# Six value products of a head in one run, six transposed-probability buffers, one move of y per head

## What is computed

```
mod = silu(cond) @ w_ada + b_ada                      # six vectors of 1024 per conditioning vector
h = rmsnorm(x, norm1) * (1 + sc1) + sh1
proj = h @ w_in                                       # columns for groups A, B, C, D
y_a = gated width-3 convolution
y_b = softmax attention, 4 latent heads (keys of width 96)
y_c = softmax attention, 4 heads on 2 key heads, with rotary tables
y_d = the same, in a window of 128 tokens, with a sink in the denominator
x = x + g1 * (concat(y_a, y_b, y_c, y_d) @ w_out)
h = rmsnorm(x, norm2) * (1 + sc2) + sh2
x = x + g2 * (gated MLP with a width-3 convolution on h)
```

## Time and profile before

| what | value |
|---|---|
| median of 3 runs | 1806.75 us (1806.15 to 1808.81) |
| the profiled execution: time, span | 1807.65 us, 1805.9 us |
| granted TensorE clock, mean | 0.981 |
| PE busy | 1712.2 us (95%) |
| PEld busy | 1537.8 us (85%) |
| DVE busy | 1114.8 us (62%) |
| ACT busy | 626.3 us (35%) |
| POOL busy | 150.2 us (8%) |
| HBM | 86 GB/s over the span |

### The profile page before, as it was taken

One profiled execution on the slowest core, in us unless ns is written; L12 is line 12 of the kernel. 1 busy time (PEld: TensorE's weight loads), 2 busy tenths in 40 slices (PEclk: granted clock), 3 DMA queues, 4 the chain that ended last, 5 costly groups with the idle time before them and its releaser, 6 DMA issues.

```text
span 1805.9 us, 30070 instructions
## 1 busy us (share of the span) xinstructions
PE 1712.2 (95%) x11625; PEld 1537.8 (85%) x11625; DVE 1114.8 (62%) x2279; ACT 626.3 (35%) x1257; POOL 150.2 (8%) x152
## 2 busy tenths in 40 slices
PE   5899999899999999999989989979999999999997
PEld 3899555469999999999989965545999999999997
DVE  3656666565766566566782856656576565665675
ACT  2421453453432222322242235436243322222223
POOL 0351010120000000000004402011100000000000
PEclk7899999999999999999999999999999999999998
DMA  8331442332222222222312322212223222222211
GB/s 273 110 103 36 143 146 94 117 120 68 71 82 70 80 71 70 81 70 80 89 47 67 95 78 94 94 48 87 89 70 94 71 70 74 77 70 81 70 59 59
DMA packets 188438, 156.53 MB, mean 87 GB/s; under 512 B 7824, under 2 KB 175284, under 8 KB 188340
## 3 DMA queue, kind: packets, MB, share of 16 engines
q1 hardware_dynamic: 188340, 155.19, 28.1%
HBM read 151.86 MB, written 3.31 MB: 86 GB/s over the span
## 4 chain that ended last, share of the span: by engine, by line
PE 85%; DVE 6%; DMA 3%; ACT 3%; issue 2%; POOL 1%; SPq 0%; DVEq 0%; ACTq 0%
PE PS L1106 81%; PE PS L1110 4%; DMA RW<-in_w_ada_dram 2%; DMA RW<-in_w_in_dram 1%; DVE H_lo L1627 1%; POOL SS L762 1%; DVE H_lo L1876 1%; DVE QTR L1566 1%; DVE X L1676 0%; ACT PT L781 0%; DVE ST L1827 0%; ACT H_hi L781 0%; POOL W_lo L740 0%; DVE XN_b L1614 0%; DVE KTR L1566 0%
## 5 line engine op out<-in xcount | busy, mean ns | idle before, releaser
L1106 PE MATMUL PS<-H_hi,W_lo 128*128 128x384 f32 (+1 forms) x1728 | 416.7, 310 | 0.0
L1106 PE MATMUL PS<-H_hi,W_hi 128*128 128x384 f32 (+1 forms) x1728 | 416.5, 310 | 0.0
L1106 PE MATMUL PS<-H_lo,W_hi 128*128 128x384 f32 (+1 forms) x1728 | 416.4, 310 | 0.0
L1106 PEld LDWEIGHTS PS<-H_lo,W_hi 128*128 128x128 f32 x1728 | 275.7, 189 | 0.0
L1106 PEld LDWEIGHTS PS<-H_hi,W_lo 128*128 128x128 f32 x1728 | 275.6, 189 | 0.0
L1106 PEld LDWEIGHTS PS<-H_hi,W_hi 128*128 128x128 f32 x1728 | 274.7, 189 | 0.8 <-issue 0.8
L781 ACT ACTIVATE W_hi<-RW 128x1024 fp32r<-128x1024 f32 (+1 forms) x176 | 183.9, 1050 | 190.1 <-PE PS L1106 161.7
L1945 DVE TENSOR_SCALAR CF<-U,VT 128x644 f32<-128x644 f32 x88 | 49.0, 556 | 268.7 <-ACT U L781 268.4
L1106 PE MATMUL PS<-G_hi,W_hi 128*128 128x384 f32 (+1 forms) x704 | 171.7, 310 | 0.0
L1106 PE MATMUL PS<-G_lo,W_hi 128*128 128x384 f32 (+1 forms) x704 | 171.4, 310 | 0.0
L1106 PE MATMUL PS<-G_hi,W_lo 128*128 128x384 f32 (+1 forms) x704 | 170.6, 308 | 0.0
(11 more groups left out here) (170 smaller groups left out, 2438.2 us busy)
## 6 DMA issues: line engine op xcount, KB each, us to landing
RW<-in_w_ada_dram SPq DMA_DIRECT2D x96, 512.0 KB, 4.4
RW<-in_w_up_dram SPq DMA_DIRECT2D x88, 512.0 KB, 3.8
RW<-in_w_down_dram SPq DMA_DIRECT2D x44, 512.0 KB, 3.6
RW<-in_w_in_dram SPq DMA_DIRECT2D x28, 512.0 KB, 3.9
RW<-in_w_out_dram SPq DMA_DIRECT2D x16, 512.0 KB, 3.4
RW<-in_w_in_dram SPq DMA_DIRECT2D x8, 352.0 KB, 3.2
out_dram<-OUT SPq DMA_DIRECT2D x5, 512.0 KB, 3.1
XIN<-in_x_sample_dram SPq DMA_DIRECT2D x4, 512.0 KB, 6.5
```

What stands on the lines that cost most here:

```text
L1106: return nc.tensor.matmul(out, lhsT, rhs, start=start, stop=stop, skip_group_check=True)
```

## The change

1. In `attention_order` the six V of head h-1 follow each other, behind the K and Q transposes of head h+1, instead of one after each score step. For head 7 and the last head they follow the transposes of their own probabilities.
2. The head's chunks (one or two) follow directly behind these V, the second chunk no longer between S(h, 3) and S(h, 4).
3. Transposed probabilities have six buffers (`turned`): PT's two and PT_ctx, PT_more (two) and PT_last, in gaps of the layout.
4. The prompt's part of y goes to the other half of the columns of bank 6, so all six products are in the bank together. A new event "Y" moves both parts behind the last V; PE waits for y_lo once a head.
5. DVE divides the last query tile's probabilities after the K and Q copies, not at once.

The chunks are the same in number and order, and RW still has three buffers.

```
--- before.py
+++ after.py
@@ -186,38 +186,32 @@
     chunks, two = list(chunks), len(chunks) // HEADS + bool(len(chunks) % HEADS)
     assert two == 2
     late = []
+
+    def moved(h):
+        return [("Y", h, TT), ("Y", h, QT)]
     for h in range(HEADS):
         t, v = probs(h - 1) if h else ([], [])
+        todo = [("ADA", chunks.pop(0)) for _ in range(
+            1 + (len(chunks) > HEADS - h if h % 3 == 0 else len(chunks) >= 2 * (HEADS - h)))]
         if h == 8:
-            order += t[:1] + late + t[1:2]
-            for x in range(2, len(t)):
-                order += v[x - 2:x - 1] + t[x:x + 1]
-            order += v[-2:]
+            order += late + moved(h - 2) + t + v + moved(h - 1)
             t, v, late = [], [], []
         if h == 0 or kv_of(h) != kv_of(h - 1):
             order += [("T", ("K", kv_of(h), 0)), ("T", ("K", kv_of(h), 1))]
-        order += late + [("T", ("Q", h, 0)), ("T", ("Q", h, 1))]
+        order += [("T", ("Q", h, 0)), ("T", ("Q", h, 1))]
         if h == 3:
             order.append(("PREP", 1))
-        todo = [chunks.pop(0) for _ in range(1 + (len(chunks) > HEADS - h if h % 3 == 0 else len(chunks) >= 2 * (HEADS - h)))]
-        order += [("ADA", todo[0])] + t[:1]
+        order += late + (moved(h - 2) if late else []) + todo + t[:1]
         for q in range(NQ):
             order.append(("S", h, q))
-            order += t[q + 1:q + 2] + v[q:q + 1]
+            order += t[q + 1:q + 2]
             if h == 7:
                 order += mla[3 * q:3 * q + 3]
-            if q == 3 and len(todo) > 1:
-                order.append(("ADA", todo[1]))
-        late = v[5:]
+        late = v
         if h == 7:
             order += mla[15:] + [("PREP", 2)]
     t, v = probs(HEADS - 1)
-    order += late + t[:1] + [("MOVE",)] + t[1:2]
-    for x in range(2, len(t)):
-        order += v[x - 2:x - 1] + t[x:x + 1]
-        if x == 3:
-            order.append(("SEL",))
-    order += v[-2:]
+    order += late + moved(HEADS - 2) + t[:2] + [("MOVE",)] + t[2:5] + [("SEL",)] + t[5:] + v + moved(HEADS - 1)
     assert not chunks
     return order
 
@@ -280,12 +274,15 @@
         w.close()
 
         CQ = sb("CQ", [P, 2, 3, P])
-        sb("W_hi_0", [P, RMAX - 6 * P])
+        PT_ctx = sb("PT_ctx", [P, P])
+        sb("W_hi_0", [P, RMAX - 7 * P])
         R = sb("R", [P, 512])
-        sb("W_hi_1_to_3", [P, 3 * RMAX - 512])
+        PT_last = sb("PT_last", [P, NLAT])
+        sb("W_hi_2_to_3", [P, 2 * RMAX])
         TAP = sb("TAP", [P, 2, 4 * HD])
         TBP = sb("TBP", [P, 2, 4 * HD])
-        sb("W_lo_1_to_3", [P, 3 * RMAX])
+        PT_more = sb("PT_more", [P, 2, NLAT])
+        sb("W_lo_2_to_3", [P, 2 * RMAX])
         K = sb("K", [P, K_N])
         VT = sb("VT", [P, DEPTH, 72 + 132])
         MOD = sb("MOD", [P, 48, 2])
@@ -460,12 +457,17 @@
                 return PR[:, h % 2, c0:c0 + P * (1 + hi - lo)]
             return PR[:, h % 2, c0:c0 + P + NLAT].rearrange("p (b n) -> p b n", n=HALFK)
 
+        def turned(i):
+
+            return (PT_ctx, PT[:, 0, :], PT[:, 1, :], PT_more[:, 0, :], PT_more[:, 1, :], PT_last)[i % 6]
+
         def y_parts(k, r0):
 
 
+
             if k == TT:
-                return [(r0, 0, CTX0, CTX0 + P)]
-            return [(HD * x, QHALF * x, QHALF * x, QHALF * (x + 1)) for x in range(2)]
+                return [(r0, QHALF - 4 * r0, CTX0, CTX0 + P)]
+            return [(HD * x, QHALF * x, QHALF * x, QHALF * (x + 1)) for x in (1 - r0 // HD, r0 // HD)]
 
         def values_done(eng, l, i):
 
@@ -483,10 +485,10 @@
             if kind == "P":
                 _, h, k = key
                 i = 6 * h + P_SEQ.index(k)
-                if i >= 2:
-                    values_done(eng, l, i - 2)
+                if i >= 6:
+                    values_done(eng, l, i - 6)
                 c0, c1 = (0, P) if k == TT else (P * queries(h, k)[0], P * queries(h, k)[1])
-                copy(PT[:, i % 2, c0:c1], bank[:, c0:c1]).then_inc(done, 1)
+                copy(turned(i)[:, c0:c1], bank[:, c0:c1]).then_inc(done, 1)
             elif kind == "Q":
                 _, h, part = key
                 if h >= 2:
@@ -968,13 +970,15 @@
                     elif e == ("V", HEADS - 1, 0):
                         item(l, NPROJ)
                         item(l, NPROJ + 1)
-                    elif e[0] == "V" and e[2] in (TT, QT):
+                    elif e[0] == "Y":
                         h, k = e[1:]
                         i, r0, tile = 6 * h + P_SEQ.index(k), HD * (h % 2), YTILE[h // 4] + h % 4 // 2
-                        values_done(act, l, i)
-                        for p0, b0, c0, c1 in y_parts(k, r0):
+                        values_done(act, l, 6 * h + TT)
+                        for x, (p0, b0, c0, c1) in enumerate(y_parts(k, r0)):
+                            if k == QT and x == 1:
+                                act.wait_ge(y_lo, l * (3 * HEADS) + 3 * h + 1)
                             copy(H_hi[r0:r0 + HD, tile, c0:c1], PS[p0:p0 + HD, 6, b0:b0 + c1 - c0]).then_inc(y_hi, 1)
-                    if waiting and (e[0] == "V" or e[0] == "MOVE"):
+                    if waiting and (e[0] in ("V", "MOVE") or e[0] == "T" and e[1][0] in ("P", "Q")):
                         exponentials(*waiting)
                         waiting = None
 
@@ -1360,17 +1364,17 @@
                         i, r0 = 6 * h + P_SEQ.index(k), HD * (h % 2)
                         m_ = FILL_AT[("P", h, k)]
                         pe.wait_ge(tr_ev[m_ % 2], l * NEV[m_ % 2] + (m_ // 2 + 1))
-                        yi = 3 * h + (k != TT)
-                        if k in (TT, 0) and yi:
-                            pe.wait_ge(y_lo, l * (3 * HEADS) + yi)
+                        if k == TT and h:
+                            pe.wait_ge(y_lo, l * (3 * HEADS) + 3 * h)
                         kv = kv_of(h) - 4 if h >= 8 else kv_of(h) % 2
                         tile = {TT: QT, 0: PAST}.get(k, k - 1)
                         c0, c1 = (0, P) if k == TT else (P * queries(h, k)[0], P * queries(h, k)[1])
                         if h == 8 and k == TT:
                             all_moved(pe, l, "MV")
                         for x, a0, a1 in value_parts(h, k):
-                            mm(PS[HD * x:HD * (x + 1), 6, a0:a1], v_ap(h // 4, kv, tile), PT[:, i % 2, a0:a1],
-                               k in (TT, 0), k in (TT, QT)).then_inc(pv_mm[x], 1)
+                            b0 = y_parts(k, HD * x)[0][1] if k == TT else a0
+                            mm(PS[HD * x:HD * (x + 1), 6, b0:b0 + a1 - a0], v_ap(h // 4, kv, tile),
+                               turned(i)[:, a0:a1], k in (TT, 0), k in (TT, QT)).then_inc(pv_mm[x], 1)
                     elif e[0] == "ADA":
                         if e[1] == ATT_ADA[l][0] and l + 1 < DEPTH:
                             pe.wait_ge(v_ev, l + 2)
@@ -1852,11 +1856,11 @@
                         if waiting:
                             normalise_probs(*waiting)
                         waiting = e[1:]
-                        if e[2] == QT:
-                            normalise_probs(*waiting)
-                            waiting = None
                         continue
                     if e[0] == "T" and e[1][0] == "P" and waiting and waiting[0] == e[1][1]:
+                        normalise_probs(*waiting)
+                        waiting = None
+                    if e[0] == "V" and waiting and waiting[1] == QT:
                         normalise_probs(*waiting)
                         waiting = None
                     if e[0] == "T" and not by_scalar(e[1]):
```

## The result

| | before | after |
|---|---|---|
| median of the runs (4 each) | 1807.53 us | 1853.63 us |
| lowest to highest | 1806.15 to 1808.81 | 1850.9 to 1857.37 |
| span of the profiled execution | 1805.9 us | 1851.7 us |
| mean granted clock | 0.981 | 0.968 |

The ratio is 1.0257, 95% interval [1.0237, 1.0277]: 2.6% slower, 46 us, as forecast to within a microsecond. The sum was right; whether its terms were is another question, which the experiments answer for the large ones.

What follows compares the result with a forecast made beforehand. It took PE's program and waits to bound the kernel. Terms -19.2 + 43.2 - 2.2 + 17.0 + 9.0 + 2.9 - 4.5 gave +46.2 us on 1807.65, forecast 1853 us, 2.6% slower; range near 1822 to 1880.

Steps and rivals of the forecast that it cites:

- The stalls: At 16 chunk pairs, PE waits 3.0 us each for the fourth half's weights: 48.0 us, +43.2 beyond today's waits.
- The clock: Behind the pairs' stalls the granted clock halves in 12 of 16 places at 1.7 us, less 3.4 existing: +17 us.
- Values in one run: Attention's value products, grouped, take 0.43 us instead of 0.59; 120 joints of 0.16 save 19.2 us.
- a step without a value product: Inner score step takes 1.70 us on PE; DVE and ACT just fit, PE has no slack, so 0 counted.
- Block ahead of head 8: Six values fill the 1.93 us hole behind head 7's preparation: -2, and -2.5 for the clock.
- The end of a layer: POOL's two splits of 2.3 us each follow the last head's transposes, fewer PE interruptions: 0, ends +2 or -2.
- K and Q copies: Q's transposes wait longer for DVE's copy at five heads of each layer, 0.9 us more in ten places: +9.
- head 8's chunk was free: Head 8's second chunk, hidden by an exponential before, costs its 1.0 us ahead of the scores, three places: +2.9.
- The clock didn't stay up: Rival behind the pairs' stalls: the clock mostly stays up, the 20.4 us fall away, 1833 us; chance 0.20.
- the stalls were not 3.6 us each: Rival at the pairs: slower transfers, +9.6 us, and drops everywhere, about +15 on the clock: 1878 us; chance 0.15.
- the faster case: Rival at the value groups: all visible PEld idle returns, 66 us, clock and K copies cost nothing: 1777 us; chance 0.03.
- the fourth half is not requested ahead of PE's first: Denies the rival that early requests remove the pairs' wait: near 1800 us or no change; chance 0.02.

Runs made afterwards that it cites:

- Experiments 3 and 6: 3: changed kernel, only each pair's fourth half moved behind the fourth score step, 1780.13 us; 6: changed kernel, values and y's move between a pair's two chunks, 1820.53 us.
- experiment 1: Changed kernel with only the pairs undone, a head's second chunk back behind the fourth score step: 1780.82 us, ratio 0.983 to the kernel before.
- Experiment 4: Changed kernel with ten dummy identity products between the third and fourth half of each pair: 1835.67 us, ratio 1.013 to the kernel before.
- experiment 5: experiment 1 with a head's six late values moved from behind the Q transposes to ahead of them: 1771.83 us, ratio 0.9782 to the kernel before.
- experiment 7: experiment 1 with a value product behind each score step again, the sixth behind the next Q transposes: 1797.69 us, ratio 0.993 to the kernel before.
- experiment 9: experiment 7 with values again interleaved between transposes ahead of head 8 and behind the last head: 1803.91 us, ratio 0.9967 to the kernel before.

## Why the prediction was right, and where only its sum was

Four steps between kernels, in microseconds, with the 95% interval as "to either side". The first holds everything but the grouping and the pairs:

| step | ratio from, to | us | to either side |
|---|---|---|---|
| six buffers, y once a head, order of DVE and of a head's start | 1, 0.9967 | -6 | 2 |
| values together in the four blocks | 0.9967, 0.993 | -7 | 4 |
| values together behind a head | 0.993, 0.983 | -18 | 7 |
| chunks in pairs | 0.983, 1.0257 | +77 | 7 |
| all | 1, 1.0257 | +46 | 4 |

**The stalls were right, and are the cause.** Sixteen waits, 45.5 us where 48.0 stood in the sum, 2.8 us each instead of 3.0. The single observation in the earlier trace rows, 4.51 us from a half to the one that reuses its buffer, gave it: the changed kernel shows 4.63, the dummy products 4.77 and the values inside the pair 4.48. Experiments 3 and 6 show the mechanism, not only the amount. One half moved removes the wait, and work placed ahead of it uses most of the time: values there left waits of 0.2 to 0.9 us.

**The clock was right in kind; how near the size was, the runs can't tell.** The forecast had 17 us: 12 drops of 16, 20.4, less 3.4 that exist. The clock fell behind ten stalls, not 12. Layer 0, with eight of them, was busy for 16.5 us more than in experiment 1. Experiment 4 measured 23 us, some 7 to either side, which is 1.4 us a pair or 2.3 for each of the ten. The Trainium skill (TensorE: Matmul & The Clock Gate, "Loop structure matters more than you think") has PE go cold behind a long wait for a DMA. Taken for these stalls of 2.0 to 3.4 us, as the forecast took it, that would mean a drop behind all 16, and 27 us. The trace agrees in ten; behind three stalls that began at full clock it stayed up. The 23 us alone could not decide.

**Values in one run: the amount was right, two of its reasons were not.** The forecast's 19.2 us were 120 joints of 0.16. Twenty of the 24 heads stand in the third row of the table, 16 us by that price, 18 measured; four stand in the second, 3.2. The 0.43 us of a product inside the run is there to the digit, but the last one takes 0.74 (in experiment 5, ahead of transposes, 0.73, 232.66 to 233.39). The 0.75 us a head are 0.15 a joint.

That a step without a value product takes 1.70 us was right only in size: 1.66. The reason given, that PE has no slack, was wrong. PE alone needs 1.52 us (222.91 to 224.43): scores behind transposes start 0.44 us after them (223.99 to 224.43) where the values took 0.52, and scores take 1.08 (222.91 to 223.99) where they took 1.18. The scores that start at 226.18 and 229.55 wait for the exponential, and each of these two steps took 1.75 us. The engines that bound an inner step are now ACT and DVE. The forecast put their chain at 3.3 us for two steps, 1.67 each; its own rows give 218.57 + 0.80 + 0.19 = 219.56 less 216.14, that is 3.42 and 1.71. Two steps of the changed kernel take 3.27 to 3.37. So PE gained 0.18 us a step that the forecast did not have, and most of it went into that wait.

**Block ahead of head 8: right in sum.** Forecast -4.5 for the hole and its clock, and 3.2 of the joints, 7.7; the second row of the table measured 7, some 4 to either side. The end of a layer was counted as 0. Over the whole profile PE's waits for W_lo, POOL's splits, are 6.5 us in the changed kernel and were 3.8, so it cost some 3.

**K and Q copies: the amount right, the cause half right.** The forecast put +9 on Q's transposes, waiting for KTR in ten places. In the changed kernel those ten waits are 5.6 us, against 2.6 before, so the wait that it named grew by 3 and not by 9. The 3.9 us for QTR are gone. What grew most is the wait for ACT's copy of the last transposed tile, 10.3 us in 16 places, which a value product had covered. Over the whole profile KTR, QTR and PT_last are 14.8 + 0 + 10.3 us against 11.4 + 3.9 + 0, +9.8. At one head with new keys:

```profile
250.97 0.44 PE L1114 MATMUL PS<-K,KS 128*128 128x128 f32 x2 [0.73 <-ACT PT_last L783]
251.86 0.77 PE L1114 MATMUL PS<-K,QS 128*128 128x128 f32 x5 [0.46 <-DVE KTR L1570]
```

The wait for ACT comes ahead of the wait for KTR and hides a part of it. In experiment 7 a value product again covers ACT's copy, and nothing stands between K's and Q's transposes. There Q's wait at such a head is 0.77 us (234.37), where the kernel before has 0.19; the forecast took 1.1. The step that failed is the sentence "Q's waited 0.19 us more for DVE's copy", taken for the whole of the exposure: it looked at the copy behind a transpose and not at the bank ahead of it, which the transposes share with the probabilities.

**What the sum left out, or let cancel.** The pairs had 43.2 - 2.2 + 2.9 and 17 on the clock, 61 us, and cost 77. The rest had -19.2 + 9.0 - 4.5, that is -15 us, and gave -31. So the sum came out to the microsecond by luck: the pairs were 16 us too cheap, and everything else 16 us too dear.

Of the pairs' missing 16, 6 are the clock if experiment 4's 23 us are taken as they stand. Another 5 are the waits for PT_last: over the whole profile 5.4 us with the chunks apart and 10.3 in pairs. A chunk behind the fourth score step gave ACT 1 us more ahead of the copy. It covered the exponentials too, which is the "head 8's chunk was free" term for all heads; waits for PR are 6.5 and 9.3 us, 3 more. The last 2 us, and how the 16 divide, are less than the intervals can tell. On the other side stand the first row of the table, which had 0 and gave -6, and the copies, which had 9. KTR, QTR and PT_last together are 15.3 us before, 19.3 in experiment 1 and 25.1 in the changed kernel: 4 of the 9.8 belong to the change without the pairs, and the others count among the pairs' 77. What the last 5 us of the 16 are is open.

**The rivals.** The clock didn't stay up; the stalls were not 3.6 us each; the joint gave 0.15 and not the 0.55 us from which the faster case starts; the fourth half is not requested ahead of PE's first. The faster case was nearer than its chance of 0.03 says in one sense only: with one half moved, the same change is 1.7% faster.

**What stays open.** Why pairs cost 59 us in the kernel before and 77 in the changed one was not tried apart. In layer 0 the traces put it on idle PE, 32.1 us more in one case and 40.0 in the other, while the busy time grows by 17.5 and 16.5; the waits for PT_last and PR are 6.0 of it in the changed kernel (from 1.6 + 1.9 to 5.2 + 4.3) and 0.8 in the other (PR alone, from 1.9 to 2.7). That score steps without values give ACT less time is argued from the waits, not shown. A fourth raw buffer, the direct test of the ring, was not built. Whether the 6 us of the first row come from the buffers, from y, from the order of DVE, or from a drop of the clock that happens not to be in that kernel's profile (before, 0.72 from 192.10 on the earlier trace rows; in experiment 9, 1.00 from 190 to 200) was not tried either. The last value product's new place costs something inside them: KTR and QTR waits are 17.6 us in experiment 9 and 15.3 before.

## What to carry to other kernels

Count how many loads a run of consecutive consumers needs and compare it with the ring: with three buffers the fourth consumer in a row waited for a load that began when the first was done, and started 4.5 to 4.8 us behind the first, whatever the mean DMA share said (0.39 in layer 0's stage before the change). Where such a run can't be split, put work into it that must be done anyway, and best of all move only the last consumer: one half of a chunk, moved in 16 places, here turned a loss of 2.6% into a gain of 1.7%. When work is taken out from between two steps, list for each engine what it covered, the copies out of shared banks among it; the next bound here was a copy of the last tile and not the one that was looked at.

## What the runs showed of the hardware that was not expected

- Ten useless products (twenty instructions) a stall made the kernel 23 us faster, some 7 to either side: the stage of layer 0 fell from 249.44 to 230.51 us at a clock of 1.00 in place of 0.92.
- Scores behind transposes start 0.44 us after the transposes do, value products behind the same transposes 0.52 to 0.53 us, though the transposes are the same four instructions of 0.60 us (223.99 to 224.43; 224.59 to 225.12 in experiment 7). By the Trainium skill (TensorEngine Tiling, "Key Properties") a change of tiling mode drains the engine; the 0.08 us ahead of the values fit that, and so does the 0.43 us of a product inside a run against 0.59 alone. The last product of a run takes 0.73 to 0.74 us, so grouping saves 0.75 us for six and not five times 0.16 exactly. The page names no price; these rows do.
- A PE that was idle for 1.65 us (317.34, experiment 7) kept its full clock in the next 10 us, where the kernel before lost it after 1.93 us at 317.85. The length alone doesn't decide: in the changed kernel it was kept after 3.13 us (222.18) and lost after 2.75 (238.65).
